# Attention units in a two-layer block: three under way instead of two, and one batch of filling per unit

## The chip, the cores and the metric

The kernel runs on 1 core of one Trainium2 chip. The metric is device time in microseconds (us); before the change it is 2705.35 us, the median of 3 runs (2704.01 to 2706.07). About 0.2% (5.4 us) is what a measurement of this kernel tells from no change.

## The reference

The input is 512 tokens with 16 meta tokens ahead of them (528 rows, width 1024). Two layers each run three branches (a pooling mixer, differential attention, a recurrent mixer), gate and merge them, and add a feed-forward part; a further block with a mixture of experts follows. All is in float32. The attention of one layer, cut to what matters here:

```python
def diff_attention(q, k, v, lam, lambda_init, subln_w):   # 4 heads, 2 score maps of width 64 per head, v of width 128
    chunk = (jnp.arange(Lp) - N_META) // CHUNK
    def block(args):
        qi, ci = args
        s = jnp.einsum('bqhcd,bkhcd->bhcqk', qi, k).astype(jnp.float32) * scale
        mask = chunk[None, :] <= ci[:, None]
        s = jnp.where(mask, s, -jnp.inf)
        p = jax.nn.softmax(s, axis=-1)
        a = p[:, :, 0] - lam * p[:, :, 1]
        return jnp.einsum('bhqk,bkhe->bqhe', a.astype(v.dtype), v)
```

The gates of a layer are `sigmoid(h @ w_gate)` with 3 x 1024 columns; they depend on nothing in the attention.

## The kernel before

Five programs are written out by hand, one for each engine, and tied by semaphores. An engine does its own instructions in the order of its program. Large products are taken in three passes of a rounded float32 kind (high times high, high times low, low times high), so every slab of weights (128x1024) needs a high part, cast by ScalarE (`high_parts`, L300), and a low part, a subtraction by VectorE or GpSimd (`low_parts`, L311). The gates' slabs have theirs made by GpSimd.

Attention goes over 20 units, u = 0 to 19: unit u is (query tile j, head h) with j = u // 4; tile 0 has 16 rows, the others 128. Unit u sees 16, 144, 272, 400 or 528 keys, for j = 0 to 4. A unit's steps are:

- scores(u), TensorE, into PSUM banks 0-1 or 2-3 by turns; for j = 4 into all of 0-3.
- mask, maximum (L1602) and shift (L1609), VectorE.
- two exponentials with their sums (L1512), ScalarE, into EE[u % 2].
- reciprocal, weight, scaling (L1615) and combination (L1620, step "ab") into AB[u % 2], VectorE.
- turned(u): j+1 transposes on TensorE (L1425) into banks 4 and 5; ScalarE copies them to AT (L1491, L1493).
- summed(u): j+1 products of AT with the values, TensorE, into bank 4; ScalarE copies that to BD (L1527, step "bd"). The next turned must wait for this copy, since it writes banks 4 and 5 again.

Into this TensorE weaves other work of the layer, above all the gates (`fill_pe`). One fill step is 6 matmuls of 264 columns (258 in the second layer). A gate is 8 steps: 4 for bank 6, 4 for bank 7. The loop of TensorE in iteration u is: scores(u), fill(2), turned(u-1), fill(2), summed(u-1). Each call of fill on TensorE is matched by one call on the other engines, in the order of their programs. On ScalarE such a call first takes the tanh of each half gate which that TensorE call finished (L612; after a second half it also issues the store to DRAM, L616), and then casts the high parts of further slabs (L300). ScalarE's iteration u before is: fill, turned(u-1), exponentials of u, fill, copy bd(u-1). Fill calls in the attention loop start at the boundary of a gate half, so the four steps of one iteration finish one half gate; a new slab is begun in every second iteration.

Of the kernel before, what the change touches and what calls it, by code (L numbers as in the profile page):

```python
# [14 lines left out]
T = 528  # L15
TILES = [(0, 16), (16, 128), (144, 128), (272, 128), (400, 128)]
# [1346 lines left out]
UNITS = [(j, h) for j in range(5) for h in range(4)]  # L1363
# [7 lines left out]
def attention_pe(k, e, w, l, fill):  # L1371
    s, banks = k.s, k.banks
    P, V, A = s["att_pe"], s["att_dve"], s["att_act"]
    for m in range(8):
        sl = k.slabs.use(("qk", l, m), [("w_in", (l,), 0, 8, (4 + m) * 128, 128)], ("att_pe", (l, "qk", m)))
        b = banks.place(w, (l, "qk", m), 2)
        w.wait_ge(*k.ready(sl))
        project(k, e, k.views(sl)[0], 0, k.hx, b).then_inc(*P.done((l, "qk", m)))
        banks.emptied_by(b, 2, "att_act", (l, "raw", m))
    for half in range(2):  # L1380
        for kh in range(2):
            sl = k.slabs.use(("v", l, half, kh), [("w_in", (l,), 4 * kh, 4, 1536 + half * 256, 256)],
                             ("att_pe", (l, "v", half, kh, 4)))
            w.wait_ge(*k.ready(sl))
            wv = k.views(sl)[0]
            for j, (t0, n) in enumerate(TILES):
                if kh == 0:
                    banks.await_empty(w, j)
                for q in range(4):
                    ins = mm3(e, k.PS[:, j, 0:256], k.hx(4 * kh + q, t0, 128), (wv[0][:, q, :], wv[1][:, q, :]),  # L1390
                              kh == 0 and q == 0, kh == 1 and q == 3)
                ins.then_inc(*P.done((l, "v", half, kh, j)))
                if kh:
                    banks.emptied_by(j, 1, "att_act" if j % 2 else "att_dve", (l, "v", half, j))

    banks.await_empty(w, 5)
    w.wait_ge(*V[l, "lp"])
    mm(e, k.PS[:, 5, 0:2], k.c("one"), k.lp, True, True).then_inc(*P.done((l, "lambda")))
    banks.emptied_by(5, 1, "att_act", (l, "lambda"))

    def scores(u):
        j, h = UNITS[u]
        t0, n = TILES[j]
        nk = t0 + n
        b, nb = score_banks(u)
        width = nk // (nb // 2)
        banks.await_empty(w, b, nb)
        w.wait_ge(*V[l, "rotated", 7])
        for x in range(nb // 2):
            for c in range(2):  # L1410
                part = slice(64 * c, 64 * c + 64)
                ins = mm(e, k.PS[0:n, b + c * (nb // 2) + x, 0:width], k.Qf[part, h, t0:t0 + n],
                         k.KK[part, h, x * width:x * width + width], True, True)
        ins.then_inc(*P.done((l, "scores", u)))
        banks.emptied_by(b, nb, "att_act", (l, "exp", u))

    def turned(u):
        j, h = UNITS[u]
        n = TILES[j][1]
        banks.await_empty(w, 4, 2)  # L1420
        w.wait_ge(*V[l, "ab", u])
        for kt in range(j + 1):
            k0, kn = TILES[kt]
            out = k.PS[0:kn, 5, 0:n] if kt == 0 else k.PS[0:kn, 4, (kt - 1) * 128:(kt - 1) * 128 + n]
            ins = e.transpose(out, k.AB[u % 2][0:n, k0:k0 + kn], k.c("id")[0:n, 0:n])  # L1425
        ins.then_inc(*P.done((l, "turned", u)))

    def summed(u):
        j, h = UNITS[u]
        t0, n = TILES[j]  # L1430
        w.wait_ge(*A[l, "at", u])
        w.wait_ge(*A[l, "v", 1, 3])
        w.wait_ge(*V[l, "v", 1, 4])
        for kt in range(j + 1):
            kn = TILES[kt][1]
            ins = mm(e, k.PS[:, 4, 0:n], k.VTa[0:kn, kt, h * 128:h * 128 + 128], k.AT[u % 2][0:kn, kt, 0:n],
                     kt == 0, kt == j)
        ins.then_inc(*P.done((l, "summed", u)))
        banks.emptied_by(4, 2, "att_act", (l, "bd", u))

    for u in range(len(UNITS) + 1):
        if u < len(UNITS):
            scores(u)
        if u:
            fill(2 if u < len(UNITS) else 5)
            turned(u - 1)
            fill(2)
            summed(u - 1)
    fill(4)
    for h in range(4):  # L1450
        b = banks.place(w, (l, "subln", h), 2)
        w.wait_ge(*A[l, "square", h])
        colsum(k, e, k.c("one"), k.Qf[:, h], b).then_inc(*P.done((l, "subln", h)))
        banks.emptied_by(b, 2, "att_act", (l, "subln", h, "log"))
    for x in range(12):
        fill(3)


def attention_act(k, e, w, l, fill):
    s, at = k.s, k.banks.at  # L1460
    P, V, A = s["att_pe"], s["att_dve"], s["att_act"]
# [13 lines left out]
    for half in range(2):  # L1475
        for kh in range(2):
            high_parts(k, e, w, k.slabs.index["v", l, half, kh] + AHEAD)
        for j in (1, 3):
            n = TILES[j][1]
# [7 lines left out]
    def turned(u):  # L1487
        j, h = UNITS[u]
        n = TILES[j][1]
        w.wait_ge(*P[l, "turned", u])  # L1490
        ins = e.copy(k.AT[u % 2][0:16, 0, 0:n], k.PS[0:16, 5, 0:n])  # L1491
        if j:
            ins = e.copy(k.AT[u % 2][:, 1:j + 1, 0:n], k.PS[:, 4, 0:128 * j].rearrange("p (a t) -> p a t", a=j))  # L1493
        ins.then_inc(*A.done((l, "at", u)))

    def soft(u):
        j, h = UNITS[u]
        t0, n = TILES[j]
        nk, i = t0 + n, u % 2
        b, nb = score_banks(u)  # L1500
        hb = nb // 2
        width = nk // hb
        sc = k.SC[:, 16 * i:16 * i + 16]
        if u >= 2:
            w.wait_ge(*V[l, "ab", u - 2])
        w.wait_ge(*V[l, "shift", u])
        for c in range(2):
            src, dst = k.PS[0:n, b + c, 0:width], k.EE[i][0:n, c * T:c * T + nk]
            if hb == 2:
                src = k.PS[0:n, b + c * hb:b + c * hb + hb, 0:width]  # L1510
                dst = dst.rearrange("p (a b) -> p a b", a=2)
            ins = e.activation(dst, src, ACT.Exp, bias=sc[0:n, 6 + c:7 + c], scale=0.125,  # L1512
                               accum_out=sc[0:n, 8 + c:9 + c])
        ins.then_inc(*A.done((l, "exp", u)))

    for u in range(len(UNITS) + 1):
        if u:
            fill()
            turned(u - 1)
        if u < len(UNITS):  # L1520
            soft(u)
        if u:
            j, h = UNITS[u - 1]
            t0, n = TILES[j]
            fill()
            w.wait_ge(*P[l, "summed", u - 1])
            e.copy(k.BD[:, h, t0:t0 + n], k.PS[:, 4, 0:n]).then_inc(*A.done((l, "bd", u - 1)))  # L1527
    w.wait_ge(*A[l, "bd", len(UNITS) - 1])
    for h in range(4):
        e.activation(k.Qf[:, h], k.BD[:, h], ACT.Square).then_inc(*A.done((l, "square", h)))  # L1530
# [16 lines left out]
def attention_dve(k, e, w, l, fill):  # L1547
    s, at = k.s, k.banks.at
    P, V, A, G = s["att_pe"], s["att_dve"], s["att_act"], s["att_pool"]
# [24 lines left out]
    for half in range(2):  # L1574
        for kh in range(2):
            low_parts(k, e, w, "lo_dve", k.slabs.index["v", l, half, kh] + AHEAD)
        for j in (0, 2, 4):
            n = TILES[j][1]
# [9 lines left out]
    def soft(u):  # L1588
        j, h = UNITS[u]
        t0, n = TILES[j]  # L1590
        nk, i = t0 + n, u % 2
        b, nb = score_banks(u)
        width = nk // (nb // 2)
        sc = k.SC[:, 16 * i:16 * i + 16]
# [10 lines left out]
        if nb == 4:  # L1605
# [8 lines left out]
        w.wait_ge(*V[l, "weight", u])  # L1614
        e.tensor_scalar(k.EE[i][0:n, T:T + nk], k.EE[i][0:n, T:T + nk], sc[0:n, 12:13], None, MUL).then_inc(  # L1615
            *step("second"))
        if u >= 2:
            w.wait_ge(*P[l, "turned", u - 2])
        w.wait_ge(*V[l, "second", u])
        e.scalar_tensor_tensor(out=k.AB[i][0:n, 0:nk], in0=k.EE[i][0:n, 0:nk], scalar=sc[0:n, 10:11],  # L1620
                               in1=k.EE[i][0:n, T:T + nk], op0=MUL, op1=SUB).then_inc(*step("ab"))

    for u in range(len(UNITS) + 1):
        if u:
            fill()
        if u < len(UNITS):
            soft(u)
        if u:
            fill()
    fill()  # L1630
    e.tensor_scalar(k.sub, k.col("da_subln", 0, l), 1.0 - linit, None, MUL).then_inc(*V.done((l, "scale")))
    w.wait_ge(*V[l, "scale"])
    for h in range(4):
# [12 lines left out]
def attention_pool(k, e, w, l, fill):  # L1646
    s = k.s
    w.wait_ge(*s["post_dve"][l, "out", 3])
    for i in range(2):
        e.memset(k.rot_qk[i], 0.0).then_inc(*s["att_pool"].done((l, "zero", i)))  # L1650
    for m in range(8):
        raw = k.raw_qk[m % 2]
        w.wait_ge(*s["att_act"][l, "raw", m])
        if m >= 4:
            w.wait_ge(*s[f"swap{m % 2}"][l, m, 72])
        e.tensor_tensor(k.Qf[:, m] if m < 4 else raw, raw, k.c("cos"), MUL).then_inc(*s["att_pool"].done((l, "cos", m)))
    for u in range(2 * len(UNITS) + 13):
        fill()


# [2252 lines left out]
def memory(nc, ctx, k):  # L3913
# [17 lines left out]
    tiles = lambda x, n=8: x.rearrange("p (k t) -> p k t", k=n)  # L3931
# [36 lines left out]
    o = 12864  # L3968

    def buf(n=512):  # L3970
        nonlocal o
        o += n
        return A[:, o - n:o]
# [20 lines left out]

    o = 2112
    k.BD, k.Qf = tiles(buf(2112), 4), tiles(buf(2112), 4)
    k.KK = tiles(buf(4224)[:, 0:2112], 4)
    k.KN, k.VTa = tiles(buf(2112), 4), tiles(buf(2560), 5)
    k.raw_qk, k.rot_qk = [buf(T) for _ in range(2)], [buf(T) for _ in range(2)]
    k.EE, k.AB = [buf(1056) for _ in range(2)], [buf(T) for _ in range(2)]  # L4000
    k.AT = [tiles(buf(640), 5) for _ in range(2)]
    k.SC = buf(64)
    k.lam, k.lp, k.le = k.small[:, 40:41], k.small[:, 41:43], k.small[:, 43:45]
# [29 lines left out]
    o = 0  # L4033
# [183 lines left out]
```

## Time and profile before

| | us |
|---|---|
| median of 3 runs | 2705.35 |
| the profiled execution's own time | 2706.09 |
| its span | 2703.9 |
| TensorE matmul busy | 2646.0 (98%) |
| TensorE weight load busy | 2417.2 (89%) |
| VectorE busy | 1823.1 (67%) |
| ScalarE busy | 1134.5 (42%) |
| GpSimd busy | 353.1 (13%) |

The attention loops stand at about 382 to 488 us (first layer) and 1416 to 1521 us (second layer) from the span's start. The times of two neighbouring starts on TensorE say how long the first of them holds the engine; the listed duration of a matmul is longer, since matmuls are pipelined. The 2.2 us between span and own time lie around the span.

### The profile page before, as it was taken

The page shows a single profiled execution, that of the slowest core. Times are in us where ns is not written, and L with a number is a line of the kernel's source. Part 1 is how long each engine was busy: PE and PEld are TensorE (multiplying, and loading weights), DVE is VectorE, ACT ScalarE, POOL GpSimd, SP SyncE. Part 2 cuts the span into 40 slices and gives each one's busy share as a digit, 9 for nine tenths or more (in the row PEclk, how much of TensorE's full clock was granted, in tenths as well). Part 3 has the DMA queues.
Part 4 walks back from the last instruction along what each step waited for, and adds up shares of the span by engine and source line. Part 5 has one row for each costly group of instructions (what it writes and reads, how often), then busy time and mean ns, then how long its engine had stood idle before and what let it go on. Part 6 is the DMA issues. An engine that isn't in the chain of part 4 may idle for free.

```text
span 2703.9 us, 55964 instructions
## 1 busy us (share of the span) xinstructions
PE 2646.0 (98%) x24551; PEld 2417.2 (89%) x24551; DVE 1823.1 (67%) x2786; ACT 1134.5 (42%) x1844; POOL 353.1 (13%) x217
## 2 busy tenths in 40 slices
PE   8999999999999999999999999999999999999998
PEld 7988998999999999988898899999987788877886
DVE  7744345556888746934335555888836998887887
ACT  6333335524333324423324624333323345466664
POOL 1211122230111000211122221111100000010001
PEclk9999999999999999999999999999999999999999
DMA  4211322364343343211232263334332322399996
GB/s 149 75 50 35 98 84 65 118 195 148 125 135 124 133 139 108 86 50 35 77 93 77 75 191 122 118 125 141 116 115 75 107 81 99 144 384 386 396 392 253
DMA packets 114203, 373.19 MB, mean 138 GB/s; under 512 B 13072, under 2 KB 14240, under 8 KB 113568
## 3 DMA queue, kind: packets, MB, share of 16 engines
q1 hardware_dynamic: 88848, 303.97, 33.2%
q10 hardware_dynamic: 18592, 41.92, 4.4%
q0 software_dynamic: 6512, 23.62, 2.4%
q8 instruction: 197, 3.23, 0.5%
q14 instruction: 54, 0.44, 0.1%
HBM read 336.44 MB, written 31.94 MB: 136 GB/s over the span
## 4 chain that ended last, share of the span: by engine, by line
PE 84%; DVE 10%; ACT 3%; DMA 1%; issue 1%; POOL 0%; SPq 0%; DVEq 0%; ACTq 0%; POOLq 0%
PE PS L316 83%; DMA RING<-wts 1%; DVE ARENA L1218 1%; DVE ARENA L846 1%; DVE HR L482 1%; DVE RINGR L311 1%; ACT ARENA L408 0%; PE PS L3270 0%; PE PS L1425 0%; DVE ARENA L848 0%; DVE H L492 0%; DVE ARENA L813 0%; ACT ARENA L410 0%; DVE ARENA L815 0%; DVE WR L3259 0%
## 5 line engine op out<-in xcount | busy, mean ns | idle before, releaser
L316 PE MATMUL PS<-HR,HIGHR 128*128 128x264 f32 (+1 forms) x2976 | 845.1, 284 | 0.0
L316 PEld LDWEIGHTS PS<-HR,HIGHR 128*128 128x128 f32 x2976 | 561.3, 189 | 0.8
L316 PE MATMUL PS<-XR,HIGHR 128*128 128x264 f32 (+2 forms) x1760 | 546.1, 310 | 6.0 <-ACT STAGE L612 5.3
L300 ACT CAST HIGHR<-RING 128x1024 fp32r<-128x1024 f32 (+2 forms) x340 | 330.7, 977 | 289.9 <-DMA RING<-wts 111.1
L316 PE MATMUL PS<-XR,RINGR 128*128 128x264 f32 (+1 forms) x1568 | 445.5, 284 | 0.0
L316 PE MATMUL PS<-HH,HIGHR 128*128 128x264 f32 (+2 forms) x1472 | 424.4, 288 | 2.9 <-DVE RINGR L311 1.4
L316 PE MATMUL PS<-HH,RINGR 128*128 128x264 f32 (+2 forms) x1472 | 421.4, 286 | 0.0
L311 DVE TENSOR_TENSOR RINGR<-RING,HIGHR 128x1024 fp32r<-128x1024 f32 (+2 forms) x272 | 311.3, 1149 | 118.0 <-ACT HIGHR L300 118.0
L316 PEld LDWEIGHTS PS<-XR,HIGHR 128*128 128x128 f32 x1760 | 331.8, 189 | 39.4 <-issue 19.4
L316 PE MATMUL PS<-ARENA 64*64 64x64 f32 (+10 forms) x7946 | 296.9, 240 | 12.3 <-DVE ARENA L1218 2.9
L316 PEld LDWEIGHTS PS<-XR,RINGR 128*128 128x128 f32 x1568 | 296.5, 189 | 0.0
L316 PEld LDWEIGHTS PS<-ARENA 64*64 64x64 f32 (+6 forms) x7946 | 250.9, 137 | 49.7 <-issue 8.7
L316 PEld LDWEIGHTS PS<-HH,HIGHR 128*128 128x128 f32 x1472 | 277.7, 189 | 8.0 <-issue 6.3
L311 POOL TENSOR_TENSOR RINGR<-RING,HIGHR 128x1024 fp32r<-128x1024 f32 x68 | 168.1, 2473 | 861.2 <-ACT HIGHR L300 861.2
L316 PEld LDWEIGHTS PS<-HH,RINGR 128*128 128x128 f32 x1472 | 278.0, 189 | 1.4
L1954 ACT COPY ARENA<-PS 128x528 f32<-128x528 f32 (+1 forms) x86 | 51.3, 596 | 320.1 <-PE PS L316 319.9
L2025 DVE SCALAR_TENSOR_TENSOR ARENA<-ARENA,COLS 128x528 f32<-128x528 f32 (+1 forms) x176 | 172.4, 979 | 6.2
L316 PE MATMUL PS<-WH,UBR 128*128 128x256 f32 (+1 forms) x680 | 170.2, 329 | 0.0
L316 PE MATMUL PS<-FL,HIGHR 128*128 128x264 f32 (+1 forms) x528 | 169.3, 321 | 0.0
L3259 DVE TENSOR_TENSOR WR<-ARENA,WH 128x1024 fp32r<-128x1024 f32 x119 | 142.1, 1219 | 24.2 <-ACT WH L3250 24.2
L3250 ACT CAST WH<-ARENA 128x1024 fp32r<-128x1024 f32 x119 | 119.8, 1055 | 62.3 <-DVE RING L3532 62.3
L316 PE MATMUL PS<-FH,HIGHR 128*128 128x264 f32 (+1 forms) x432 | 139.4, 323 | 0.0
(446 smaller groups left out, 5134.4 us busy)
## 6 DMA issues: line engine op xcount, KB each, us to landing
RING<-wts SPq DMA_DIRECT2D x324, 512.0 KB, 3.6
ARENA<-wmoe SPq DMA_DIRECT2D x204, 512.0 KB, 6.8
RING<-wts SPq DMA_DIRECT2D x52, 256.0 KB, 3.1
gates<-STAGE ACTq DMA_DIRECT2D x48, 264.0 KB, 4.3
ARENA<-gates ACTq DMA_DIRECT2D x48, 264.0 KB, 2.9
ys<-RING ACTq DMA_DIRECT2D x16, 512.0 KB, 7.1
RING<-wts SPq DMA_DIRECT2D x16, 384.0 KB, 3.1
ys<-STAGE POOLq DMA_DIRECT2D x8, 512.0 KB, 6.1
```

Of the source, the lines that this page charges most:

```text
L300: e.copy(k.highR[:, hs, 0:n], k.ring[:, i % NRING, 0:n]).then_inc(*k.s["hi"].done(i))
L311: e.tensor_tensor(k.ringR[:, i % NRING, 0:n], k.ring[:, i % NRING, 0:n], k.highR[:, hs, 0:n].bitcast(F32), SUB).then_inc(*k.s[name].done(i))
L316: return e.matmul(out, lhsT, rhs, start=start, stop=stop, skip_group_check=True)
L482: e.tensor_tensor(k.HR[:, q, cols], k.scaled[st[0]](q)[:, cols], high(q)[:, cols].bitcast(F32), SUB).then_inc(*k.s["part_dve"].done(key + ...
L846: e.tensor_tensor(k.dif[i % 2], r[:, 0:T], r[:, 1:529], SUB).then_inc(*V.done((l, "dif", i)))
L1218: e.tensor_tensor(cut(dst), src, mask(m, 2, 4), MUL).then_inc(*V.done(key(name)))
L1954: e.copy(k.tv(k.RW[f % 2][p][:, 2 + FIRST[l]:530], T - FIRST[l]), k.pv(at["up", l, f, p], T - FIRST[l])).then_inc(*A.done((l, "raw", f, p)))
L2025: e.scalar_tensor_tensor(out=cv[:, own], in0=r[:, T - n + q:T + q], scalar=tap(q), in1=cv[:, own], op0=MUL, op1=ADD).then_inc(*V.done((l, ...
L3250: e.copy(high, raw).then_inc(*k.s["moe_act"].done(("high", g)))
L3259: e.tensor_tensor(low, raw, high.bitcast(F32), SUB).then_inc(*k.s["moe_dve"].done(("low", g)))
```

## The change

Three buffers for the exponentials (EE), the combined weights (AB) and their scalars (SC) take the place of two, in memory that lay unused behind KK. turned and summed are now those of the unit two before, so three units are under way. The fill steps of an iteration are one call of 4 in place of two calls of 2, and iterations 0 and 1 have none (before, iteration 1 had one pair). After the loop the last two units are finished with fill(3), fill(3), fill(3), fill(2) between their parts (before: fill(5), fill(2)). The number of fill steps in the attention loop is 83 both before and after. ScalarE's fill call stands ahead of the copy bd(u-2); the other call of an iteration, ahead of turned, is gone. The banks of PSUM stay as they were: one place (4 and 5) for turned and summed.

```diff
@@ attention_pe
-            ins = e.transpose(out, k.AB[u % 2][0:n, k0:k0 + kn], k.c("id")[0:n, 0:n])
+            ins = e.transpose(out, k.AB[u % 3][0:n, k0:k0 + kn], k.c("id")[0:n, 0:n])
...
-    for u in range(len(UNITS) + 1):
-        if u < len(UNITS):
-            scores(u)
-        if u:
-            fill(2 if u < len(UNITS) else 5)
-            turned(u - 1)
-            fill(2)
-            summed(u - 1)
+    last = len(UNITS) - 1
+    for u in range(last + 1):
+        scores(u)
+        if u >= 2:
+            turned(u - 2)
+            fill(4)
+            summed(u - 2)
+    for u in (last - 1, last):
+        fill(3)
+        turned(u)
+        fill(last + 2 - u)
+        summed(u)
@@ attention_act
-        if u >= 2:
-            w.wait_ge(*V[l, "ab", u - 2])
+        if u >= 3:
+            w.wait_ge(*V[l, "ab", u - 3])
...
-    for u in range(len(UNITS) + 1):
-        if u:
-            fill()
-            turned(u - 1)
-        if u < len(UNITS):
-            soft(u)
-        if u:
-            j, h = UNITS[u - 1]
-            t0, n = TILES[j]
-            fill()
-            w.wait_ge(*P[l, "summed", u - 1])
-            e.copy(k.BD[:, h, t0:t0 + n], k.PS[:, 4, 0:n]).then_inc(*A.done((l, "bd", u - 1)))
+    def emptied(u):
+        j, h = UNITS[u]
+        t0, n = TILES[j]
+        fill()
+        w.wait_ge(*P[l, "summed", u])
+        e.copy(k.BD[:, h, t0:t0 + n], k.PS[:, 4, 0:n]).then_inc(*A.done((l, "bd", u)))
+
+    last = len(UNITS) - 1
+    for u in range(last + 1):
+        if u >= 2:
+            turned(u - 2)
+        soft(u)
+        if u >= 2:
+            emptied(u - 2)
+    for u in (last - 1, last):
+        fill()
+        turned(u)
+        emptied(u)
@@ attention_dve
-        if u >= 2:
-            w.wait_ge(*P[l, "turned", u - 2])
+        if u >= 3:
+            w.wait_ge(*P[l, "turned", u - 3])
...
-    for u in range(len(UNITS) + 1):
-        if u:
+    for u in range(len(UNITS)):
+        soft(u)
+        if u >= 2:
             fill()
-        if u < len(UNITS):
-            soft(u)
-        if u:
-            fill()
-    fill()
+    for u in range(5):
+        fill()
@@ memory
-    k.KK = tiles(buf(4224)[:, 0:2112], 4)
+    k.KK = tiles(buf(2112), 4)
+    third = [buf(1056), buf(T)]
+    o += 528
...
-    k.EE, k.AB = [buf(1056) for _ in range(2)], [buf(T) for _ in range(2)]
+    k.EE, k.AB = [buf(1056) for _ in range(2)] + third[:1], [buf(T) for _ in range(2)] + third[1:]
```

## Rows read from the trace of the kernel before

**Rows 1.** The page: the chain that ended last, by engine.
```profile
PE 84%; DVE 10%; ACT 3%; DMA 1%; issue 1%; POOL 0%; SPq 0%; DVEq 0%; ACTq 0%; POOLq 0%
```

**Rows 2.** Windows: start:end, length, busy (instructions) by engine, clock, DMA share, GB/s.
```profile
0.00:8.00 8.00, 2.04 (x5) 1.66 (x6) 0.53 (x5) 2.46 (x3) 0.20 (x4) 1.00 0.77 247
...
382.00:490.00 108.00, 107.24 (x800) 93.54 (x799) 58.85 (x148) 52.16 (x171) 23.77 (x10) 1.00 0.24 69
1416.00:1524.00 108.00, 107.13 (x806) 93.60 (x805) 58.92 (x148) 52.53 (x172) 23.83 (x10) 1.00 0.23 69
```

**Rows 3.** TensorE in time at the loop's start: start, us, what [idle before].
```profile
384.96 0.17 PE L1425 MATMUL PS<-CST,ARENA 16*16 16x16 f32 x1 [0.69 <-DVE ARENA L1602]
...
388.64 0.28 PE L316 MATMUL PS<-XR,RINGR 128*128 128x264 f32 x1
389.00 0.17 PE L1425 MATMUL PS<-CST,ARENA 16*16 16x16 f32 x1
```

**Rows 4.** VectorE in time at the loop's start.
```profile
384.59 0.22 DVE L1620 SCALAR_TENSOR_TENSOR ARENA<-ARENA 16x16 f32<-16x16 f32 x1
...
384.95 2.38 DVE L1609 TENSOR_SCALAR ARENA<-ARENA 16x2 f32<-16x2 f32 x1
```

**Rows 5.** TensorE in time, one unit of j = 4.
```profile
469.06 0.39 PE L316 MATMUL PS<-XR,HIGHR 128*128 128x264 f32 x1
469.29 0.28 PE L316 MATMUL PS<-HR,HIGHR 128*128 128x264 f32 x1
...
470.62 0.71 PE L1425 MATMUL PS<-CST,ARENA 128*16 128x128 f32 x5
471.09 0.37 PE L316 MATMUL PS<-XR,HIGHR 128*128 128x264 f32 x1
...
472.72 0.48 PE L316 MATMUL PS<-ARENA 16*128 16x128 f32 x2
```

**Rows 6.** TensorE in time: summed with the following scores, and the next fill matmul.
```profile
390.76 0.54 PE L316 MATMUL PS<-ARENA 16*128 16x16 f32 x6
391.23 0.39 PE L316 MATMUL PS<-XR,HIGHR 128*128 128x264 f32 x1
...
398.81 0.84 PE L316 MATMUL PS<-ARENA 16*128 16x16 f32 x6
399.58 0.39 PE L316 MATMUL PS<-XR,HIGHR 128*128 128x264 f32 x1
...
402.91 1.35 PE L316 MATMUL PS<-ARENA 16*128 16x128 f32 x8
404.19 0.39 PE L316 MATMUL PS<-XR,HIGHR 128*128 128x264 f32 x1
...
412.14 1.56 PE L316 MATMUL PS<-ARENA 16*128 16x128 f32 x8
413.63 0.39 PE L316 MATMUL PS<-XR,HIGHR 128*128 128x264 f32 x1
```

**Rows 7.** ScalarE in time: tanh, store, copy to BD, cast.
```profile
387.88 0.36 ACT L612 ACTIVATE STAGE<-PS 128x264 f32<-128x264 f32 x1
388.14 0.14 ACT L1527 COPY ARENA<-PS 128x16 f32<-128x16 f32 x1
...
390.87 0.39 ACT L612 ACTIVATE STAGE<-PS 128x264 f32<-128x264 f32 x1 [0.99 <-PE PS L316]
391.29 0.32 ACTq L616 DMA_DIRECT2D gates<-STAGE  x1
391.65 0.17 ACT L1527 COPY ARENA<-PS 128x16 f32<-128x16 f32 x1 [0.39 <-PE PS L316]
...
484.31 1.05 ACT L300 CAST HIGHR<-RING 128x1024 fp32r<-128x1024 f32 x1 [0.40 <-ACT STAGE L612]
485.26 0.25 ACT L1491 COPY ARENA<-PS 16x128 f32<-16x128 f32 x1
```

**Rows 8.** GpSimd in time at the loop's start.
```profile
384.94 2.37 POOL L311 TENSOR_TENSOR RINGR<-RING,HIGHR 128x1024 fp32r<-128x1024 f32 x1 [12.06 <-ACT HIGHR L300]
```

More of the change, by code:

```diff
@@ L1498, in soft @@
         t0, n = TILES[j]
-        nk, i = t0 + n, u % 2
+        nk, i = t0 + n, u % 3
         b, nb = score_banks(u)
@@ L1590, in soft @@
         t0, n = TILES[j]
-        nk, i = t0 + n, u % 2
+        nk, i = t0 + n, u % 3
         b, nb = score_banks(u)
@@ L1656, in attention_pool @@
         e.tensor_tensor(k.Qf[:, m] if m < 4 else raw, raw, k.c("cos"), MUL).then_inc(*s["att_pool"].done((l, "cos", m)))
-    for u in range(2 * len(UNITS) + 13):
+    for u in range(len(UNITS) + 15):
         fill()
```

## The prediction

> **What bounds the kernel now.** I read the chain of waits by engine first: 84% of what ended last is TensorE [rows 1]. Then the windows of the two attention loops: TensorE is busy 107.24 and 107.13 us of 108 [rows 2]. So there is no wait of any size left to remove in the stretch that is changed: 0.8 us a layer. VectorE (58.85 of 108) and ScalarE (52.16 of 108) are half idle there [rows 2]. A version gains only if TensorE does less or waits less, and any new wait of TensorE goes straight into the end, since what follows is TensorE's too. The reader is to look, then, not at how many units are under way but at which of TensorE's waits lost the work that covered it. For that I went to the time lines of TensorE, ScalarE and VectorE through the loop.
>
> **What it removes: changes between kinds of matmul.** One iteration of j = 4 is fill(2) in 469.06 to 470.62 (1.56 us), five transposes in 0.47, fill(2) in 471.09 to 472.72 (1.63 us), then summed [rows 5]. In the first batch the first matmul holds TensorE 0.23 us and the other 11 take (470.62 - 469.29) / 11 = 0.121 each. So a batch costs about 0.10 on entry, and ahead of a product of the other kind 0.08 more on leaving (1.63 - 0.22 - 11 x 0.121). One batch of 24 is 24 x 0.121 + 0.10 + 0.08 = 3.10 us, in place of 1.56 + 1.63 = 3.19: 0.09 saved. For units of j = 0, where both batches pay both ends, it is twice that, 0.19. Before there were 39 batches after turned(0), after there are 22: 17 fewer, 3 of them at 0.19 and 14 at 0.09, together 1.8 us a layer. The transposes now follow the scores directly, and the trace shows no such pair. The bounds are one whole entry either way, 0.1 us on each of 18 (1.8 us a layer); I take nothing, since in the rows the price sits at the batches of fill, and keep both ends.
>
> **What it moves at the start.** In iteration 1 fill(2) ran while TensorE would have waited for ab(0). turned(0) starts at 384.96 after only 0.69 of idle time [rows 3]; it waits for L1620, which ends at 384.59 + 0.22 = 384.81 [rows 4]. Nothing in the change makes ab(0) earlier: scores, exponentials and VectorE's steps of unit 0 stand where they stood. So turned(0) comes at the same time, but 12 matmuls of fill that lay in that wait now lie behind it: 12 x 0.121 = 1.46 us lost a layer. The number of fill steps in the loop is the same, so this is not given back at its end. Against that, turned(1) was 0.24 late before (388.64 to 389.00, where 0.12 is usual) [rows 3], because L1609 of unit 1 stood 2.38 us [rows 4] beside GpSimd's low part of 2.37 [rows 8]; with ab a unit ahead, this goes. Without any new wait a layer thus comes to -1.8 + 1.46 - 0.24 = -0.6 us. Already that is small: most of what the joined batches bring is eaten by the first wait.
>
> **What it uncovers: the copy out of bank 4.** turned(u-1) writes banks 4 and 5 and must wait for ScalarE's bd(u-2), which waits for summed(u-2). Before, fill(2) stood between the two (1.5 us). Now only scores(u+1) does. Measured from the start of summed, TensorE comes to the next turned after summed and scores: 0.47 us for two units of j = 0 (390.76 to 391.23), 0.77 when the scores are of j = 1 (398.81 to 399.58), 1.28 with both of j = 1 (402.91 to 404.19), 1.49 with scores of j = 2 (412.14 to 413.63) [rows 6]. Later units only have more of both.
>
> What has to happen meanwhile on ScalarE, in its program's order: the tanh of the half gate, which can't start before the fourth fill step ends, that is, at the start of summed; then, in even iterations, the cast of a new slab, and in odd ones the issue of the store; then the copy bd. The prices: tanh starts 0.11 after summed starts (390.76 [rows 6], 390.87 [rows 7]); from tanh to the next instruction 0.26 (387.88 to 388.14); from a cast to the next 0.95 (484.31 to 485.26); from a tanh over its store to the copy 0.78 (390.87 to 391.65); the copy 0.17 for 16 columns [rows 7], and I take 0.1 more for 128, as the copy of 16 rows and 128 columns to AT shows 0.25 [rows 7]; from the end of an operation that TensorE waits for to TensorE 0.15 (384.81 [rows 4] to 384.96 [rows 3]). So bank 4 is free for TensorE at 0.11 + 0.26 + 0.95 + 0.17 + 0.15 = 1.64 after summed starts in even iterations, and at 0.11 + 0.78 + 0.17 + 0.15 = 1.21 in odd ones; with 128 columns at 1.74 and 1.31.
>
> The waits, iteration by iteration: u = 2: 1.64 - 0.47 = 1.17. u = 3: 1.21 - 0.77 = 0.44. u = 4: 1.64 - 0.77 = 0.87. u = 5: 0.44. u = 6: 1.74 - 1.28 = 0.46. u = 7: 1.31 is under 1.49, none. u = 8: 1.74 - 1.49 = 0.25. From u = 10 on summed and scores are long enough. The sum is 3.6 us a layer. Behind the waiting turned on TensorE stands all the rest; nobody else is held who matters, since slabs and gates go at TensorE's pace. This is the term that decides. Its bounds: if the copy were not behind tanh and cast at all, only the chain summed, copy, turned would be left, some 0.15 us at u = 2 and 0 later; if each of the tanhs came 0.3 later than I have it, five terms grow by 0.3, to 5.1, and one or two appear. I take 3.6, as each part of it has its own row.
>
> **What is hidden.** ab(u-2) has a whole iteration more than before. The exponentials' wait (two buffers) was never TensorE's. The transposes now being ahead of the batch, ScalarE copies AT while TensorE fills, and has 3.1 us for it. The end, fill(3), fill(3), fill(3), fill(2), keeps 1.6 us ahead of summed(19), as before. The new memory is at an unused place.
>
> **A rule of the Trainium skill to weigh.** The windows show a granted clock of 1.00, the 2.4 GHz level, in both loops, and also in the first 8 us, where TensorE is busy 2.04 us of 8 [rows 2]. By "TensorE: Matmul & The Clock Gate", section "HAM oscillation — how this bites in real kernels", waits that come back between groups of matmuls can send the clock to its lower level. The new waits are 0.4 to 1.2 us between batches of 3.1, far denser than those first 8 us at a clock of 1.00, so my sum has no term for it. It is the last rival below.
>
> **Sum.** A layer: -0.6 + 3.6 = +3.0; two layers +6.1 us. The profiled execution was 2706.09 (span 2703.9 and 2.2 around it), so its like would be 2712.2; the median of the runs is 0.74 below the profiled one, so I forecast 2705.35 + 6.1 = 2711.5.
>
> **Rivals.**
> - *Only the joins count (faster or the same).* ScalarE's copy is in time because the wait takes place on something that ends sooner than I read, and transposes right behind scores are cheaper by an entry: 2 x (-0.6 - 1.8) = -4.8, 2700.5; without the second part 2704.1. For it: ScalarE is idle half of the stretch. Against it: order, not load, delays the copy. It decides where bank 4 is free within 0.5 us of summed's start. Chance 0.12.
> - *The wait is there but half as long*, since the first units of the loop slip against each other (a late turned also moves the next tanh, and TensorE's ends are modelled): 2 x (-0.6 + 1.8) = +2.4, 2707.8. Chance 0.2.
> - *The chain through VectorE is late too.* Each cast lets GpSimd start a low part of 2.4 us beside which a small VectorE step stands until it ends [rows 4, 8]. If this hits L1609, the exponentials come late, tanh and copy behind them, and turned waits more, in units that I have at nothing. Nine such parts a layer at 0.4 on average: +7 on top, 2718.5. Against it: by my reading the blocked step is free again before the batch of 24 ends. Chance 0.13.
> - *The clock falls at the waits*, and matmuls of the first units take double for some microseconds in each layer: at 0.121 a matmul, 24 to 48 matmuls twice as long are 3 to 6 us a layer, 2718 to 2724. The first 8 us speak against it. Chance 0.02.
>
> **Chances.** The forecast has 0.53, with a range of its own of 2708.5 to 2715. The whole range takes in the half-long wait, part of the first rival and the start of the VectorE one: 2704 to 2718. Slower than 2710.8 (over 0.2%, about what a measurement of this kernel can tell from no change): most of the forecast and the last two, 0.52. Within 0.2%: 0.42. Faster: 0.06, the far end of the first rival.
>
> **What would show it.** In the changed kernel's profile TensorE should wait for ScalarE L1527 (the copy bd), at turned or its weight load, about six times a layer, all in the first third of the loop, the longest 1.2 us, longer in even iterations than in odd ones, and 3 to 4 us a layer in all. Its predecessor on ScalarE should be a cast of 1.05 us in the even ones. Batches should be 3.1 us from first matmul to the next product. At the start TensorE should stand idle some 2.3 us ahead of turned(0). The loops should be about 3 us longer each, and nothing after them should change. I am wrong if that wait isn't there, if the joined batch is not near 3.10, if turned(0) comes earlier, or if the stretch beyond the loops moves.

## The result, and the profile after

The changed kernel takes 2710.1 us (median of 20 runs, 2707.38 to 2716.2) against 2705.3 (20 runs, 2700.12 to 2709.07): a ratio of 1.0023, 95% interval 1.0017 to 1.0029, so 4.6 to 7.8 us slower by the ratio and 4.8 by the medians. The forecast was 2711.5 in 2704 to 2718. The profiled execution has a span of 2706.4 us, 2.5 more than before's, which taken alone would mislead; why is said below.

The attention loops, cut at the same two instructions in all kernels (from the matmuls of lambda, which stand just ahead of scores(0), to the first sum of squares behind the loop), in us of the profiled executions:

| | before, layer 1 | after, layer 1 | before, layer 2 | after, layer 2 |
|---|---|---|---|---|
| to turned(0) | 2.83 | 2.83 | 2.83 | 2.83 |
| from turned(0) on | 105.51 | 109.09 | 104.69 | 108.11 |
| whole loop | 108.34 | 111.92 | 107.52 | 110.94 |

Each loop is longer by 3.6 and 3.4 us. The chain that ended last, by engine, answers to [rows 1], and it is the same picture:

```profile
PE 84%; DVE 9%; ACT 4%; DMA 1%; issue 1%; POOL 0%; ACTq 0%; SPq 0%; DVEq 0%; POOLq 0%
```

The windows over the loops, as in [rows 2] (length, busy by engine, clock, DMA):

```profile
382.00:490.00 108.00, 102.92 (x770) 89.80 (x768) 56.05 (x148) 51.70 (x166) 22.88 (x10) 0.98 0.23 69
1416.00:1524.00 108.00, 104.34 (x780) 91.30 (x781) 55.09 (x143) 52.26 (x167) 24.12 (x10) 0.98 0.24 68
```

TensorE is no longer busy throughout: 5.1 us of 108 are idle, where 0.8 were, and the granted clock is 0.98, not 1.00. Who is waited for, in the first loop:

```profile
PEld PS L1425 <- ACT ARENA L1525: 7.7, 13, 1.2
PE PS L1425 <- ACT ARENA L1525: 3.0, 6, 1.1
PE PS L316 <- ACT ARENA L1516: 1.4, 1, 1.4
PE PS L1425 <- DVE ARENA L1612: 0.8, 1, 0.8
```

L1425 is turned, L1525 is now the copy bd (L1527 before). PEld is TensorE's weight load, which overlaps the matmuls; TensorE's own waits are the PE lines. Of these, 3.0 of 5.2 us are the forecast wait. The rest is the start: L1516 (exponentials of unit 0, for whose bank scores(2) waits) and L1612 beside ab(0).

TensorE in time, from summed(0) to turned(1), then from summed(1) to turned(2), answers to [rows 6]:

```profile
389.38 0.54 PE L316 MATMUL PS<-ARENA 16*128 16x16 f32 x6
391.00 0.18 PE L1425 MATMUL PS<-CST,ARENA 16*16 16x16 f32 x1 [1.09 <-ACT ARENA L1525]
...
394.23 0.84 PE L316 MATMUL PS<-ARENA 16*128 16x16 f32 x6
395.35 0.18 PE L1425 MATMUL PS<-CST,ARENA 16*16 16x16 f32 x1 [0.28 <-ACT ARENA L1525]
```

The same on ScalarE, to be read against [rows 7]:

```profile
389.55 0.39 ACT L612 ACTIVATE STAGE<-PS 128x264 f32<-128x264 f32 x1 [2.10 <-PE PS L316]
389.84 1.04 ACT L300 CAST HIGHR<-RING 128x1024 fp32r<-128x1024 f32 x1
390.77 0.18 ACT L1525 COPY ARENA<-PS 128x16 f32<-128x16 f32 x1
...
394.33 0.39 ACT L612 ACTIVATE STAGE<-PS 128x264 f32<-128x264 f32 x1 [2.44 <-PE PS L316]
394.76 0.32 ACTq L616 DMA_DIRECT2D gates<-STAGE  x1
395.12 0.17 ACT L1525 COPY ARENA<-PS 128x16 f32<-128x16 f32 x1 [0.39 <-PE PS L316]
```

ScalarE had waited 2.1 us for the half gate, then took tanh and cast, and only then the copy, though summed(0) had been done for about a microsecond. From summed's start to the next turned it is 1.62 in an even iteration (1.64 forecast), 1.12 in an odd one (1.21). Against the times without a wait:

| iteration | 2 | 3 | 4 | 5 | 6 | 7 | 8 | sum |
|---|---|---|---|---|---|---|---|---|
| forecast wait | 1.17 | 0.44 | 0.87 | 0.44 | 0.46 | 0 | 0.25 | 3.63 |
| measured | 1.15 | 0.35 | 0.85 | 0.35 | 0.43 | 0 | 0.22 | 3.35 |

**What I had not forecast.** The start of the loop on TensorE:

```profile
383.87 0.22 PE L316 MATMUL PS<-ARENA 64*16 64x16 f32 x4 [1.38 <-ACT ARENA L1516]
384.85 0.18 PE L1425 MATMUL PS<-CST,ARENA 16*16 16x16 f32 x1 [0.75 <-DVE ARENA L1612]
384.97 0.57 PE L316 MATMUL PS<-XR,HIGHR 128*128 128x264 f32 x1
385.34 0.42 PE L316 MATMUL PS<-HR,HIGHR 128*128 128x264 f32 x1
385.56 0.42 PE L316 MATMUL PS<-XR,RINGR 128*128 128x264 f32 x1
...
387.76 0.36 PE L316 MATMUL PS<-XR,HIGHR 128*128 128x264 f32 x1
387.96 0.28 PE L316 MATMUL PS<-HR,HIGHR 128*128 128x264 f32 x1
388.08 0.28 PE L316 MATMUL PS<-XR,RINGR 128*128 128x264 f32 x1
```

After 2.1 idle us in 2.4 (1.38 and 0.75, with the matmuls of scores(2) between) the fill matmuls come 0.22 apart instead of 0.12, for 3 us. Windows of both loops' starts say why: the granted clock is at its lower level, 1.2 GHz (0.5), for part of them.

```profile
386.00:388.00 2.00, 2.00 (x11) 2.00 (x11) 1.15 (x8) 0.61 (x4) 0.00 (x0) 0.52 0.03 8
...
1418.00:1422.00 4.00, 4.00 (x23) 3.77 (x21) 1.74 (x10) 0.86 (x6) 0.00 (x0) 0.59 0.02 4
```

The first batch takes 4.41 us, not 3.12: 1.3 us a layer. By the Trainium skill, "TensorE: Matmul & The Clock Gate", section "HAM oscillation — how this bites in real kernels", waits between groups of matmuls can bring the clock down. In this trace it fell at the idle time of the start; behind the waits of 0.15 to 1.1 us for the copy, which I had weighed, it did not fall. e4 tests whether the idle time is the cause.

**Why the profiled spans differ by 2.5 only.** I set the starts of the same ScalarE instructions of both traces side by side. The changed kernel is 3.5 us behind at 500 us, 2.5 at 560, 1.5 from 900 to 1150, then 2.1 ahead at 1250, 1.3 behind at 1530, 0.7 at 1650, 2.4 at 2360. Between 1150 and 1250 no instruction is changed; there the clock of the execution before fell twice, and that of the changed kernel did not. Before, then after:

```profile
1170.00:1180.00 10.00, 10.00 (x136) 9.24 (x135) 1.08 (x3) 0.81 (x2) 0.83 (x1) 0.83 0.04 14
1210.00:1220.00 10.00, 8.49 (x161) 7.65 (x164) 1.19 (x3) 1.66 (x3) 0.15 (x1) 0.83 0.01 4
```

```profile
1170.00:1180.00 10.00, 10.00 (x148) 8.91 (x146) 1.24 (x3) 0.97 (x2) 2.33 (x1) 1.00 0.18 66
1210.00:1220.00 10.00, 8.58 (x193) 7.59 (x191) 3.20 (x6) 2.25 (x4) 0.00 (x0) 1.00 0.02 3
```

That lies between executions, not between kernels: in the profiles of the changed kernel and its variants such falls turn up around 140 and 1170 to 1220 us in some and not in others, and around 2340 us in all, for 3 to 14 us. So an effect of a few microseconds is read from the loops; the time is read from many runs.

The 1.0 us regained by 560 in this trace is part of a wait that was already there. Before, TensorE waited twice for low parts of the branch weights; it now comes later to the same place and waits once, in this order before and after:

```profile
543.31 0.36 PE L316 MATMUL PS<-BH,HIGHR 128*128 128x264 f32 x1 [0.20 <-DVE RINGR L311]
547.35 0.36 PE L316 MATMUL PS<-PH,HIGHR 128*128 128x264 f32 x1 [0.89 <-DVE RINGR L311]
```

```profile
549.81 0.36 PE L316 MATMUL PS<-PH,HIGHR 128*128 128x264 f32 x1 [0.32 <-DVE RINGR L311]
```

This too differs between executions: in e8, the same kernel profiled again, only 0.3 us are regained there, and one wait for a low part still takes 0.9.

### The profile page after: what moved, and what is told of

Read it like the earlier page. It is cut to its first block, busy times and chain, and to the rows that moved or that the text cites. A ratio compares the mean times of both kernels' runs of the same rounds, so it can differ in the third digit from the quotient of the medians.

```text
span 2706.4 us, 55964 instructions
## 1 busy us (share of the span) xinstructions
PE 2643.6 (98%) x24551; PEld 2416.7 (89%) x24551; DVE 1816.3 (67%) x2786; ACT 1137.7 (42%) x1844; POOL 358.0 (13%) x217
## 4 chain that ended last, share of the span: by engine, by line
PE 84%; DVE 9%; ACT 4%; DMA 1%; issue 1%; POOL 0%; ACTq 0%; SPq 0%; DVEq 0%; POOLq 0%
PE PS L316 83%; DMA RING<-wts 1%; DVE ARENA L1218 1%; PE PS L1425 1%; DVE ARENA L846 1%; DVE HR L482 1%; ACT ARENA L408 0%; DVE RINGR L311 0%; PE PS L3278 0%; ACT HIGHR L300 0%; DVE ARENA L848 0%; DVE H L492 0%; DVE ARENA L813 0%; ACT ARENA L410 0%; DVE ARENA L815 0%
## 5 line engine op out<-in xcount | busy, mean ns | idle before, releaser
L316 PE MATMUL PS<-ARENA 64*64 64x64 f32 (+8 forms) x7946 | 295.7, 240 | 15.0 <-DVE ARENA L1218 2.9
L316 PEld LDWEIGHTS PS<-ARENA 64*64 64x64 f32 (+5 forms) x7946 | 250.0, 137 | 52.1 <-issue 8.5
```

Source lines behind the costliest of these rows:

```text
L316: return e.matmul(out, lhsT, rhs, start=start, stop=stop, skip_group_check=True)
```

## The experiments

Eight experiments ran; e8 is the changed kernel again. "Loop" is the length defined above, first layer and second. Theory A is the forecast with the start added: three costs, namely the copy behind tanh and cast, the fill steps taken out of the wait for ab(0), and the clock behind that idle time; and one gain, the joined batches.

| | loop | from turned(0) | first batch | waits for the copy | ratio to before, interval |
|---|---|---|---|---|---|
| before | 108.34, 107.52 | 105.51, 104.69 | 1.66, 1.63 | 0, 0 | |
| changed | 111.92, 110.94 | 109.09, 108.11 | 4.41, 4.30 | 3.0, 2.5 | 1.0023, 1.0017 to 1.0029 |
| e1 | 108.95, 106.68 | 106.12, 103.85 | 4.46, 3.03 | 0, 0 | 1.0001, 0.9990 to 1.0011 |
| e2 | 107.14, 106.39 | 104.31, 103.57 | 3.12, 3.07 | 0, 0 | 0.9996, 0.9985 to 1.0007 |
| e3 | 112.71, 112.03 | 109.04, 108.41 | 3.15, 3.06 | 2.7, 2.7 | 1.0037, 1.0023 to 1.0050 |
| e4 | 110.71, 109.78 | 107.85, 106.92 | 3.14, 3.07 | 2.9, 2.8 | 1.0042, 1.0028 to 1.0056 |
| e5 | 105.95, 105.20 | 103.13, 102.38 | 3.11, 3.07 | 0, 0 | 0.9967, 0.9955 to 0.9980 |
| e6 | 107.35, 106.57 | 103.47, 102.75 | 1.66, 1.64 | 0, 0 | 0.9993, 0.9984 to 1.0002 |
| e7 | 128.60, 129.24 | 125.08, 125.77 | 3.15, 3.06 | 0, 0 | 1.0152, 1.0137 to 1.0168 |
| e8 | 112.15, 112.07 | 109.33, 109.25 | 4.61, 5.45 | 2.8, 2.5 | 1.0013, 1.0004 to 1.0023 |

(The waits of this table are the idle times that the profile lists; by start times they are 0.06 us larger each, so 3.35 in place of 3.0. The list leaves out idle times under 0.15 us: e1, e2 and e5 have one of 0.11 in each loop, ahead of turned(1), and in both loops of e8 and the second of the changed kernel, e3 and e4 one or two of nearly 0.15 are missing from the sum.)

**e1: the copy ahead of the fill call.**

```diff
     def emptied(u):
-        fill()
         w.wait_ge(*P[l, "summed", u])
         e.copy(k.BD[:, h, t0:t0 + n], k.PS[:, 4, 0:n]).then_inc(*A.done((l, "bd", u)))
+        fill()
```

> The changed kernel, with one order swapped on ScalarE: the copy of summed out of bank 4 stands ahead of the fill call (tanh, store, cast) instead of behind it. Lengths are TensorE's, from the lambda matmuls to the first sum of squares behind the loop: 111.9 us in the first layer of the changed kernel, 108.3 before. Theory A (the copy is late because tanh and cast stand ahead of it): the waits of turned for the copy, 3.35 us in the first layer, fall to under 0.5, the loop to 109.0 +- 0.3, the time by about 6 us against the changed kernel, to within 0.1% of before. Rival B (the wait is the round trip TensorE, ScalarE, TensorE itself, whatever stands ahead): they stay over 2 us, the loop at 111 or more. Rival C (late tanhs then hold the banks of the gates): the wait reappears at fill matmuls, behind the gates' tanh.

The listed waits are gone. ScalarE around the same copy in e1:

```profile
394.13 0.17 ACT L1524 COPY ARENA<-PS 128x16 f32<-128x16 f32 x1 [2.53 <-PE PS L316]
394.19 0.40 ACT L612 ACTIVATE STAGE<-PS 128x264 f32<-128x264 f32 x1
394.48 1.04 ACT L300 CAST HIGHR<-RING 128x1024 fp32r<-128x1024 f32 x1
```

The round trip that rival B makes the cause fits within the 0.77 us of summed and scores in every later iteration. Only ahead of turned(1), where 0.47 us are covered, does it leave a wait: 0.3 us by start times in the first layer and 0.2 in the second. No wait for ScalarE appears at the fill matmuls of the loops either, so rival C fails. In the second layer the clock did not fall (first batch 3.03): that loop, with all costs gone but the lost fill, is 0.84 shorter than before; my sum without waits had said 0.6. In the first it fell, and 108.95 is the expected 109.0.

**e2: two fill steps back at the start.**

```diff
         scores(u)
+        if u == 1:
+            fill(2)
         if u >= 2:
```

> The changed kernel with a call of 2 fill steps in iteration 1, as the kernel before has one, ahead of turned(0). Two things follow: TensorE has work in the wait for ab(0), and the batches of 4 no longer end with a half gate, but 2 steps (1.46 us) behind it. Theory A (start idle time, a fall of the clock behind it, and tanh and cast at the end of the batch are the three costs): clock 1.00 in the first batch, first batch 3.1 us instead of 4.4, waits for the copy under 0.5 us in all; first loop 107.6 +- 0.5 with 2 steps (1.5 us) more in it, so 2.3 us a layer better than before; time 0.1 to 0.2% below before. Rival B (round trip alone): waits for the copy stay over 2 us, loop over 109.5. Rival D (what the joined batches save is given back behind the loops, where low parts of weights are waited for): loop as in A, time within 0.05% of before.

The loop is 107.14 with its two extra steps: as expected, and rival B is dead. But the time is not 0.1 to 0.2% lower; 1.0000 lies in the interval. With two steps more, the pooling branch's part of the fill reaches TensorE two steps earlier behind the loop, and it waits there for ScalarE's copy L620, which stands behind the normalisation:

```profile
PE PS L316 <- ACT ARENA L620: 1.7, 1, 1.7
PE PS L316 <- ACT ARENA L408: 0.9, 1, 0.9
PE PS L316 <- ACT STAGE L612: 0.4, 1, 0.4
```

These are 3.0 us from 470 to 560 us; in the changed kernel the same stretch has 1.8, and L620 is not among them. So something was given back behind the loop, but not in the low parts, as rival D had it. e5 takes this apart.

**e3: four fill steps at the start,** the same edit with `fill(4)`.

> The changed kernel with a call of 4 fill steps in iteration 1, so that TensorE has work in the wait for ab(0) but the batches still end with a half gate. Theory A: clock 1.00 in the first batch (3.1 us instead of 4.4); turned(0) about 0.8 later; waits for the copy 2.9 us (the units with a cast are now the odd ones: 0.65, 0.85, 0.35, 0.85, 0, 0.2); first loop 111.0 with 4 steps (2.9 us) more in it, thus within 0.3 of before once these are taken off; time within 0.1% of before. Rival B (round trip alone): the same waits in even and odd units. Rival E (the clock's fall has nothing to do with the idle time at the start): the clock is at 0.5 in the first batch as before.

Clock and first batch are as theory A says (3.15 and 3.06, no fall), and so is the pattern of waits: 0.58, 0.78, 0.29, 0.78, 0, 0.15, 0, 0.15 for iterations 2 to 9, with the long ones now in the odd iterations, where the cast is. Rival B has no reason for that. The loop (112.71) and the time missed by 1.7 us and 0.3%: shifted by four steps, the pooling part of the fill enters the loop's end, where one wait for L620 costs 1.72 us in each layer, and others follow behind it (6.1 us in four, over both layers).

```profile
PE PS L1425 <- ACT ARENA L1527: 2.7, 6, 0.8
PE PS L316 <- ACT ARENA L620: 1.7, 1, 1.7
```

**e4: the idle time filled with matmuls that do nothing.**

```diff
         scores(u)
+        if u in (1, 2):
+            banks.await_empty(w, 5)
+            for _ in range((0, 4, 3)[u]):
+                mm(e, k.PS[:, 5, 0:128], k.c("id"), k.c("one"), True, True)
```

> The changed kernel with 7 matmuls (128x128, float32, identity times ones, into bank 5, results not used) in the wait for ab(0): 4 behind scores(1), 3 behind scores(2). They do no work of the kernel. Theory A (the fall of the clock in the first batch comes from TensorE's idle time ahead of it): turned(0) at the same distance from the loop's start (2.6 us), clock 1.00 in the first batch, which takes 3.1 us instead of 4.4; loops 1.3 us shorter than the changed kernel's, waits for the copy as there (3.35); time 0.1% below the changed kernel. Rival E (the clock falls by chance, or by something else in the attention): still 0.5 in the first batch in both layers, loops as in the changed kernel.

The clock stays at 1.00, with turned(0) where it was (2.86), and the first batch is 3.14 and 3.07. The loops are 1.2 us shorter than the changed kernel's, which is the clock's share, by itself. The waits for the copy are unchanged, so they did not bring it down. The time, however, came out 0.2% higher, not 0.1% lower: the kernel is longer by 14 matmuls and their moves, and its trace has 7.3 us of TensorE waiting for "issue" (five times, two of them over 2 us, outside the loops) where the changed kernel has 2.6. That difference, 4.7 us, is about as large as the 0.2%, but it stands in one trace; that the added instructions cause it is not shown.

**e5: the start filled, the rest of the order kept.** e2's edit, and two steps fewer at the loop's end, so that the loop has 83 fill steps again:

```diff
     for u in (last - 1, last):
-        fill(3)
+        fill(3 if u < last else 2)
         turned(u)
-        fill(last + 2 - u)
+        fill(2)
         summed(u)
```

> The changed kernel with a call of 2 fill steps in iteration 1, and 2 steps fewer at the loop's end (fill 3, 2, 2, 2 there instead of 3, 3, 3, 2), so that every matmul behind the loop stands where it stands in the kernel before. Theory A: turned(0) at 2.83 us, clock 1.00, no waits for the copy; from turned(0) on 104.31 (this with 2 steps more) less 1.5 = 102.8 in the first layer, 102.1 in the second, against 105.5 and 104.7 before: 2.7 and 2.6 us shorter loops. If nothing is given back, the time is 5 us (0.2%) below before. Rival D (given back behind the loop): the loop is that short, but the offset against before shrinks by 1 us or more between the first sum of squares and 60 us later, in waits for low parts of weights; time within 0.1%.

The loops are 2.4 and 2.3 us shorter than before (2.7 and 2.6 expected), and it is the fastest kernel here: 2697.03 us, ratio 0.9967 (0.9955 to 0.9980), 5 to 12 us below before. Rival D fails: against before, the profiled execution is 1.9 ahead at 500 us, 1.7 at 560 and 3.1 at 900. That is the version that beats both. The loops explain 4.7 us of it. The rest isn't shown to come from the edit: the mean granted clock over whole executions is 0.998 in its 6 and 0.9966 in the 22 of before, which by estimate is 4 us of 2700, and the traces place falls of the clock outside the loops (around 1213 us in before's and not in e5's). TensorE at summed(0) and turned(1) in it, against 389.38 and 391.00 in the changed kernel, and the window over the loop:

```profile
388.66 0.54 PE L316 MATMUL PS<-ARENA 16*128 16x16 f32 x6
389.31 0.18 PE L1425 MATMUL PS<-CST,ARENA 16*16 16x16 f32 x1
```

```profile
382.00:490.00 108.00, 107.34 (x814) 94.27 (x813) 52.96 (x148) 54.39 (x173) 23.73 (x10) 1.00 0.22 69
```

0.65 us lie between them. Two units of j = 0 take 0.47, so 0.18 is what summed, copy and turned need by themselves; it is under the profile's limit, and the forecast had given some 0.15 for it. Tanh and cast are done before the batch ends, as the half gate is complete 2 steps earlier.

**e6: three units, the batches not joined.**

```diff
         if u >= 2:
+            fill(2)
             turned(u - 2)
-            fill(4)
+            fill(2)
             summed(u - 2)
```

> Three units under way and the third buffer as in the changed kernel, but the fill steps as in the kernel before: 2 in iteration 1, then 2 ahead of turned and 2 behind it; loop's end 3, 2, 2, 2. Against e5 only the joining of the batches is taken away. Theory A (depth brings nothing but the 0.24 us of turned(1); what is to be had lies in the joined batches): loop 108.0 +- 0.4 in the first layer (108.34 before), no waits for the copy, time within 0.1% of before; e5's loop is shorter than this one's by 18 joins at 0.09 to 0.19, 1.8 to 2.3 us. Rival F (the third unit itself shortens the loop, by freeing VectorE and ScalarE): loop 106.5 or less, near e5.

107.35 and 106.57: 1.0 us shorter than before, a little under the range given. In this order two batches of 2 stand ahead of turned(0) (3.88 us), so its wait of 0.7 went, and turned(1)'s 0.24; that is all the depth brings here, and it is not rival F's. e5's loop is 1.4 us shorter still. It keeps 0.55 us of wait for ab(0) and the 0.18 at turned(1), so the joins are worth 2.1, within the 1.8 to 2.3.

**e7: the joined batch, two units.**

```diff
         if u:
-            fill(2 if u < len(UNITS) else 5)
+            fill(4 if u < len(UNITS) else 5)
             turned(u - 1)
-            fill(2)
+            if u == len(UNITS):
+                fill(2)
             summed(u - 1)
```

> The kernel before with one part of the change alone: its two units under way and two buffers stay, but the fill steps of an iteration are one call of 4 between scores(u) and turned(u-1); summed(u-1) follows turned(u-1) at once. ScalarE's order is exponentials of u, copies of turned(u-1), copy of summed(u-1), fill call. Theory A (the third unit is what lets turned stand ahead of the batch, so that the copy to AT is covered): summed(u-1) now waits for ScalarE's copies to AT, 0.4 us at j = 0 to 1.0 at j = 4, and turned(1) and others for ab; 14 to 25 us a layer longer, loops of 120 to 130 us, time 1 to 2% over before. Rival F' (one batch alone would have done): loop 106 to 108.

20 to 22 us longer loops and 1.5%, as expected. summed waits for ScalarE's copies to AT:

```profile
PE PS L316 <- ACT ARENA L1494: 15.0, 15, 1.8
PE PS L316 <- ACT ARENA L1492: 1.0, 4, 0.3
```

16 us; the clock takes more (0.96 over this loop). Not all of the 16 is the copy. In e7's order the exponentials of unit u stand ahead of the copies of turned(u-1), and from u = 8 on they hold them up in every second unit:

```profile
446.43 0.59 ACT L1513 ACTIVATE ARENA<-PS,ARENA 128x400 f32<-128x400 f32 x1
446.90 0.20 ACT L1513 ACTIVATION_READ_ACCUMULATOR ARENA<-PS,ARENA 128x1 f32 x1
447.00 0.24 ACT L1492 COPY ARENA<-PS 16x128 f32<-16x128 f32 x1
447.14 0.36 ACT L1494 COPY ARENA<-PS 128x256 f32<-128x256 f32 x1
447.55 2.75 PE L316 MATMUL PS<-ARENA 16*128 16x128 f32 x10 [1.46 <-ACT ARENA L1494]
```

In six such units the copies start 1.1 to 1.4 us after the last transpose, in the others 0.2 to 0.3; that is 5.4 of the 16 us. The other 10.6 us are waits of 0.25 to 0.8 at each unit for the copy itself, and they alone are five times what the joins bring. So the third unit has a use: it lets turned stand ahead of the one batch, which covers the copy to AT. With the order of this kernel it is the condition of the joins, not a gain by itself; two units with the copies ahead of the exponentials were not tried.

**e8: the changed kernel again.**

> The changed kernel once more, as it is, for the clock behind the idle start of the loop. Theory A: TensorE idle some 2.1 us in the 2.6 ahead of turned(0), and the clock at 0.5 for about 3 us behind it in most, not all, loops (2 of 2 in the changed kernel's profile, 1 of 2 in e1, 0 of 2 in each of the kernels that have work there); where it falls the first batch is 4.3 to 4.5 us, else 3.1. Waits for the copy 3.35 us in the first layer. Time 0.15 to 0.3% over before.

The clock fell in both loops, for longer in the second (6.8 us, first batch 5.45). In all, it fell at an idle start in 5 of 6 loops (changed 2, e8 2, e1 1 of 2), and at the start of none of the 14 loops with work there (before, e2 to e7). Each fall begins 2.3 to 4.4 us after the loop's start and lasts 3.4 us, 6.8 in the one. The ratio, 1.0013 (1.0004 to 1.0023), is at the lower side of the first measurement's and overlaps it. This profiled execution (2714.29) is the second longest of its ten; its loops are 8.4 us longer than before's, where the ratio gives 1 to 6. So the time over many executions doesn't confirm the size of the clock's share; that is known from the loops of single executions.

## Why the prediction was right

Point by point, for the first layer:

- *TensorE bounds the loop, and any new wait goes to the end.* Right: loops +3.6 and +3.4, time +4.8 by the medians.
- *Joined batches, -1.8, and the late turned(1), -0.24.* From turned(0) to summed(19) all batches took 65.10 us before and 65.54 after. The 12 matmuls more are 1.46 and the clock 1.3, so the joins with turned(1) saved 2.3, where 2.04 was forecast. A batch is 3.07 to 3.12 (3.10 forecast). That transposes behind scores cost nothing extra was right but for 0.1 us: transposes in all 5.24 before, 5.33 after.
- *The start, +1.46.* turned(0) comes at the same 2.83. Right as far as it went. I said that the fill was lost, but did not ask what 2.1 idle us do to the clock.
- *The copy out of bank 4, +3.6.* 3.35, in the forecast iterations, with the cast in even ones; e1 takes it away by an exchange of order alone. The upper bound of 5.1 was added up wrong: six terms grow by 0.3, not five, which makes 5.4. A small term that I left out is scores(2), 0.3 us, which is now done in the wait ahead of turned(0).
- *The clock, no term.* Wrong: 1.3 us a layer. I compared the new waits with the first 8 us of the kernel and looked at the waits for the copy only. That comparison was a misreading. The view of windows gives 1.00 for the first 8 us, but the trace's first record of the clock is at 8.8 us, and where there is no record the view shows 1.00. The matmuls of before's own trace say the opposite: of one kind, the first 8 take 3.41 us together and the next 24 only 5.61.

```profile
5.96 3.41 PE L316 MATMUL PS<-ARENA,CST 128*128 128x264 f32 x8 [5.96 <-ACT ARENA L418]
9.62 5.61 PE L316 MATMUL PS<-ARENA,CST 128*128 128x264 f32 x24 [0.24 <-ACT ARENA L418]
```

They start 0.44 us apart up to 8.7 us and 0.22 apart later, a factor of two as between the two levels of the clock. So the row that I held against the clock's fall, which I gave a chance of 0.02, was no evidence against it. The rival I wrote had the clock falling at the waits for the copy, 3 to 6 us; it fell at the start, which no rival named.
- *Nothing after the loops changes.* Wrong by about 1 us in the first layer and 0.6 in the second, given back where low parts were waited for anyway; in e8, the same kernel, it is 0.3 and 2.0, so a single trace doesn't size it. A further 1 us is regained between 700 and 900 us. e8 regains 0.2 there, so it isn't fixed by the kernel; e1 and e5 gain 1.3 and 1.4, and e2 and e6 nothing. What makes it differ between executions stays open.

The sum came out near, +6.1 against +4.8 (4.6 to 7.8 by the ratio). The term that decides, the copy, was right in mechanism and size. But the nearness of the total is in part luck: the missed clock and the missed give-back, 2.6 and 1.6 us over two layers, are of opposite sign.

## What to carry to other kernels

On an engine that is always busy, ask of each piece of filler what it was covering: here one call of two steps stood between the freeing and the reuse of a PSUM bank, and another stood in the first unit's latency. Where an engine does a short, urgent copy and long, patient work in one program order, put the urgent one first, or see to it that the patient one becomes ready earlier: either took 3.35 us of waits to 0.2 or 0.3, with no change of load. Moving filler also moves all that it will do later; keep the count at the end of the loop, or a gain there comes back as a wait elsewhere, as in e2 and e3.

## What the runs showed of the hardware that I had not expected

- With about 2.1 us of idle TensorE in 2.4 the granted clock fell to its lower level in 5 of 6 loops, for 3.4 us in four and 6.8 in one; with 7 matmuls of 128 columns in the same gap it stayed up in both loops of e4.
- In the first 8.7 us of the kernel matmuls start 0.44 us apart, and 0.22 later: the kernel by this sign begins at the lower level, though the view of windows says 1.00 where the trace has no record of the clock.
- In e7, with TensorE waiting 0.25 to 1.8 us at every unit, the clock fell three times in the first loop and four times in the second, for 3.4 us each; in the changed kernel it did not fall behind its six waits of 0.15 to 1.1.
- Falls of the clock also come and go between executions in stretches that no kernel changed, and two of them with what goes with them are worth 3.6 us in one trace; single executions of the kernel before lie from 2696.9 to 2709.51.
